# Score parts of 512 keys in four PSUM slots, alternated with the transposed units of a head

## The chip, the cores and the metric

The kernel runs on one core of one Trainium2 chip. The metric is the time of one execution on the device in microseconds (us). TensorE (PE, and PEld for its weight loads), VectorE (DVE), ScalarE (ACT), GpSimd (POOL) and the queue of SyncE (SP) run side by side and meet at semaphores. Each engine takes its own instructions in order.

## The reference, cut to what matters

One decoder block over 2048 tokens: a convolution branch, an attention branch and a SwiGLU feed-forward. The change is in the attention branch. There an indexer picks up to 256 keys for each query; the kernel works on all causal keys and adds a mask instead of gathering:

```
score = where(causal, sum_h w_h * relu(q_idx_h . k_idx), -inf)
idx   = top_k(score, 256)
att   = (q . k[idx]) * 64 ** -0.5 - slopes * distance      # 8 heads, one shared key/value head
p     = softmax(att);  y = p @ v[idx]
```

## The kernel before, in words

The 2048 rows are worked in four groups of 512 rows. A group is `RT` = 4 row tiles of 128 queries. For each group g there are three phases: A (projections, convolution, indexer scores), C (attention and the output projections) and F (feed-forward of the group before). `ORDER` is A0 C0 A1 F0 C1 A2 F1 C2 A3 F2 C3 F3, and PE goes through it in this order. Top-k and the first mask for C run on DVE beside F.

Phase C takes 16 pairs of heads (`PAIRS`): pair i is row tile i // 4 and heads 2(i % 4) and 2(i % 4) + 1; e = 0, 1 is the head in the pair. Row tile t of group g attends to n = 4g + t + 1 key tiles of 128 keys, so 1 to 4 in group 0 and 13 to 16 in group 3. A step (i, e) does this:

- **Scores.** PE multiplies the queries of a head with the keys (L1524 with the high part of the keys, L1525 with the low part, at most 512 keys in one matmul) into one of two score slots of two PSUM banks each (`score_bank`). `parts_of(g)` is 1, 1, 2, 2: a part is up to 1024 keys (`part_span`). PE may write part r when part r - 2 has been read (L1517).
- **Mask and minimum.** DVE reads a part, adds the mask, writes `probs` and keeps the running minimum (L1221). It is a custom instruction followed by a READ_ACCUMULATOR that writes the minimum to `first_top`, or to `mx` for the last part. A later part starts from the earlier minimum, so it waits for it.
- **Exponential.** ACT takes the whole row of keys at once, up to 2048 elements (L796), after the last part of the head.
- **Units.** The probabilities of a pair are transposed on PE in units of two key tiles for both heads (L1480, helper `transposes`), into two banks used by turns. ACT copies the unit (L783: high part), DVE subtracts (L1230: low part), and PE multiplies it with the values (L1499, L1500, helper `values`, two units behind). Transposing unit k waits until DVE is done with unit k - 2, and the first unit of a pair waits for the exponentials of both its heads (`exp_done`, L1475).
- **weigh** (L1187, L1189) is DVE's finish of a pair, three units after its last one. **mark** (L953 to L964) is five DVE steps per pair that prepare the mask of the next row tile. They come behind units, in the pairs with i % 4 <= g of the first three row tiles; such pairs are called marked below.

The units of a pair come `lag` pairs after its scores: 2 in groups 0 and 1, 1 in groups 2 and 3 (`ways`). `slots(g)` lists the units and splits those of a pair over the two steps: in group 3 four units at e = 0 and three or four at e = 1; in group 2 three, and two or three; in group 1 two, and one or two.

All three engines have this order written out. On PE and DVE a step is: all score parts of (i, e), then all units of (i - lag, e). On ACT a step is the other way round: the copies of the units of (i - lag, e) (L773 to L784), and then the exponential of (i, e) (L791 to L797).

Of the kernel before, what the change touches and what calls it, by code (L numbers as in the profile page):

```python
# [23 lines left out]
def build_block(nc, A):  # L24
# [4 lines left out]
    P = 128  # L29
# [8 lines left out]
    RT = ROWS // P  # L38
# [82 lines left out]
    with ctx:  # L121
# [31 lines left out]
        KH = sb("KH", [P, SEQ], f32r)  # L153
        KL = sb("KL", [P, SEQ], f32r)
# [44 lines left out]
        PS = ctx.enter_context(nc.psum_tensor("PS", [P, 8, 512], f32))  # L199
# [22 lines left out]
        mark_step, marked0, marked, m0_ready, m_ready, s_psum, s_masked, exp_done = sem("mark_step"), sem("first_keys_marked"), sem("keys_marked"), sem("first_mask_ready"), sem("mask_ready"), sem("s_psum"), sem("scores_masked"), sem("exp_done")  # L222
# [6 lines left out]
        y_psum, y_copied, y_added, ny_done = sem("y_psum"), sem("y_copied"), sem("y_added"), sem("ny_done")  # L229
# [21 lines left out]
        def slots(g):  # L251

            out, at = [], {}
            for i in range(PAIRS):
                n = RT * g + i // (HEADS // 2) + 1
                mid = min(n, 2 * ((n + 3) // 4))
                for half, (a, z) in enumerate(((0, mid), (mid, n))):
                    at[i, half] = range(len(out), len(out) + (z - a + 1) // 2)
                    out += [(i, k, min(2, z - k)) for k in range(a, z, 2)]
            return out, at  # L260

        PAIRS = RT * HEADS // 2

        PT_BASE = [sum(len(slots(a)[0]) for a in range(g)) for g in range(GROUPS)]

        def parts_of(g):

            return (g + 2) // 2

        PART_BASE = [sum(2 * PAIRS * parts_of(a) for a in range(g)) for g in range(GROUPS)]  # L270

# [3 lines left out]

        def part_span(b, v):

            return 1024 * v, min(1024, (b + 1) * P - 1024 * v)

        def score_bank(r):  # L280

            return PS[:, 2 * (r % 2):2 * (r % 2) + 2, :].rearrange("p a n -> p (a n)")

        def pt_end(g, i):

# [616 lines left out]
        def _(dve):  # L902
# [105 lines left out]
            for ph, g in ORDER:  # L1008
                c0 = BASE[ph, g]
                if ph == "A":  # L1010
# [81 lines left out]
                    for t, b in enumerate(blocks(g)):  # L1092
                        n = (b + 1) * P
# [78 lines left out]
                elif ph == "C":  # L1172
# [4 lines left out]
                    def weigh(k):  # L1177

                        if k < 0 or k != at[table[k][0], 1].stop - 1:
                            return  # L1180
                        i = table[k][0]
                        n = PAIRS * g + i
                        t, j = i // (HEADS // 2), i % (HEADS // 2)
                        o = PS[:, 6 + n % 2, 0:2 * P]
                        dve.wait_ge(bc_done, n + 1)

                        chained(nc.vector.tensor_tensor(out=o[0:DH, :], in0=o[0:DH, :], in1=pvl[:, n % 2, :], op=ALU.add))  # L1187
                        for e in range(2):
                            nc.vector.tensor_tensor(out=att[DH * e:DH * e + DH, j, t * P:(t + 1) * P],  # L1189
                                                    in0=PS[0:DH, 6 + n % 2, e * P:(e + 1) * P], in1=bcs[DH * e:DH * e + DH, n % 2, :],  # L1190
                                                    op=ALU.mult).then_inc(att_done, 1)
# [3 lines left out]
                    for i in range(PAIRS + lag):  # L1195

                        t, u_mark = i // (HEADS // 2) + 1, i % (HEADS // 2)
                        marking = t < RT and u_mark < U
                        step = 0
                        for e in range(2):  # L1200
                            if i < PAIRS:
                                b, h = RT * g + i // (HEADS // 2), 2 * (i % (HEADS // 2)) + e

                                top = mx[:, i % held, e:e + 1]
                                if e == 0 and i >= held:

                                    dve.wait_ge(pt_psum, pt_end(g, i - held))
                                if h == 0 and b % RT == 0:
                                    dve.wait_ge(m0_ready, (g + 1) * (g + 2) // 2)
                                elif h == 0:  # L1210
                                    dve.wait_ge(m_ready, MASK_BASE[g] + b % RT * U)
                                low = 3.0e38
                                for v in range(parts_of(g)):
                                    s, w = part_span(b, v)
                                    r = part(g, i, e, v)
                                    last = v + 1 == parts_of(g)
                                    dve.wait_ge(s_psum, r + 1)
                                    if v:
                                        dve.wait_ge(s_masked, r)
                                    out = top if last else first_top[:, e:e + 1]  # L1220
                                    nc.vector.tensor_tensor_reduce(out=prob(g, i, e)[:, s:s + w], in0=score_bank(r)[:, 0:w],  # L1221
                                                                   in1=M[:, b % RT % 2, s:s + w].bitcast(f32), scale=-2.0 ** -(h + 1),
                                                                   scalar=low, op0=ALU.add, op1=ALU.min, accum_out=out).then_inc(s_masked, 1)
                                    low = out
                            if i >= lag:
                                for k in at[i - lag, e]:

                                    w = table[k][2] * 2 * P
                                    dve.wait_ge(pt_hi, PT_BASE[g] + k + 1)
                                    nc.vector.tensor_tensor(out=pt_hl(g, k, len(table), 1, w), in0=PS[:, 4 + k % 2, 0:w],  # L1230
                                                            in1=pt_hl(g, k, len(table), 0, w).bitcast(f32), op=ALU.subtract).then_inc(pt_ready, 1)
                                    if marking and step < MARKS:
                                        mark(t, RT * g + t, u_mark, step)
                                        step += 1
                                    weigh(k - 3)
                                if e == 0:

                                    n = PAIRS * g + i - lag
                                    dve.wait_ge(exp_done, 2 * n + 2)
                                    if n >= 2:  # L1240

                                        dve.wait_ge(rsb_ready, 2 * n - 2)
                                    nc.vector.reciprocal(rs[:, n % 2, :], den[:, (i - lag) % held, :]).then_inc(recip_done, 1)
                        while marking and step < MARKS:
                            mark(t, RT * g + t, u_mark, step)
                            step += 1
# [61 lines left out]
        def _(pe):  # L1308
# [68 lines left out]
            for ph, g in ORDER:  # L1377
# [83 lines left out]
                elif ph == "C":  # L1461
# [44 lines left out]
                    for i in range(PAIRS + lag):  # L1506
                        for e in range(2):
                            if i < PAIRS:
                                t, h = i // (HEADS // 2), 2 * (i % (HEADS // 2)) + e
                                if g > 0 and t == 0 and e == 0:  # L1510
                                    pe.wait_ge(qs_in[h // 2], 16 * g)
                                lhs = QS[:, h, t * P:(t + 1) * P]
                                for v in range(parts_of(g)):
                                    r = part(g, i, e, v)
                                    s0, w0 = part_span(RT * g + t, v)
                                    if r >= PART_BASE[g] + 2:
                                        pe.wait_ge(s_masked, r - 1)  # L1517
                                    elif g > 0:

                                        pe.wait_ge(ny_done, RT * (g - 1) + r - PART_BASE[g] + 1)  # L1520
                                    for at_s in range(0, w0, 512):
                                        s, w = s0 + at_s, min(512, w0 - at_s)
                                        o = score_bank(r)[:, at_s:at_s + w]
                                        mm(o, lhs, KH[:, s:s + w], start=True, stop=False)  # L1524
                                        ins = mm(o, lhs, KL[:, s:s + w], start=False, stop=True)  # L1525
                                    ins.then_inc(s_psum, 1)
                            if i >= lag:
                                for k in at[i - lag, e]:
                                    transposes(k)
                                    values(k - 2)  # L1530
                    for k in range(len(table) - 2, len(table)):
# [69 lines left out]
```

## Time and profile before

| | |
|---|---|
| median of 3 runs | 3564.96 us (3560.70 to 3566.21) |
| profiled execution, own time | 3566.14 us |
| span in it | 3564.3 us |
| PE busy | 3234.4 us, 91% |
| DVE busy | 2203.8 us, 62% |
| ACT busy | 1188.8 us, 33% |
| attention steps of groups 0, 1, 2, 3 | 345 to 411, 1111 to 1227, 1933 to 2114, 2857 to 3101 us |

Busy times count instructions that work on data. A wait counts for the engine that waits, and "<-" names what ended it. The attention steps of the four groups are 607 us of the span. The rest is mostly PE with matmul after matmul.

### The profile page before, as it was taken

The numbers are of one execution on the slowest core, as the hardware profiler recorded it, in microseconds if no ns is written. First come the engines' busy times: TensorE is split into PE (matmuls) and PEld (weight loads), VectorE is DVE, ScalarE is ACT, GpSimd is POOL, SyncE is SP. The second block draws the span as 40 slices with busy tenths as digits, with TensorE's granted clock in tenths as the row PEclk, the third lists the DMA queues.
The fourth block names the chain that finished last, engine by engine and source line by source line (L and its number), as shares of the span: only waits on it lengthen the run. The fifth ranks groups of instructions, "written<-read, shape, count | busy, mean of one in ns | idle before, by whom it ended". The sixth has DMA issues, their size and how long they took to land.

```text
span 3564.3 us, 41835 instructions
## 1 busy us (share of the span) xinstructions
PE 3234.4 (91%) x15045; PEld 2645.7 (74%) x15045; DVE 2203.8 (62%) x3903; ACT 1188.8 (33%) x2030; POOL 715.3 (20%) x482
## 2 busy tenths in 40 slices
PE   6990799999998899999998789999999867889998
PEld 5860688778886788768887678875888756768886
DVE  1758827588606826699964972759999988720001
ACT  3341641253334641261112653127111056521111
POOL 3420210035766000001212300000221231002212
PEclk9995999999998999999999999999999989999999
DMA  6970465579995265545554035552555410255554
GB/s 216 304 236 0 170 256 201 195 230 291 289 295 181 108 233 197 183 150 193 190 198 160 25 118 224 205 185 98 197 190 196 175 48 1 106 190 195 194 190 170
DMA packets 177567, 640.15 MB, mean 180 GB/s; under 512 B 11294, under 2 KB 95306, under 8 KB 115561
## 3 DMA queue, kind: packets, MB, share of 16 engines
q1 hardware_dynamic: 160512, 574.66, 46.3%
q10 hardware_dynamic: 16872, 63.01, 4.6%
q8 instruction: 121, 1.98, 0.2%
q14 instruction: 62, 0.50, 0.0%
HBM read 476.14 MB, written 161.48 MB: 179 GB/s over the span
## 4 chain that ended last, share of the span: by engine, by line
PE 62%; DVE 17%; issue 12%; ACT 4%; DMA 2%; POOL 2%; DVEq 0%; ACTq 0%; SPq 0%; POOLq 0%
PE PS L1361 14%; PE PS L1332 13%; PE PS L1333 13%; PE PS L1334 13%; DVE probs L1221 3%; DVE flags L1127 2%; DVE W L1112 1%; DVE PT L1230 1%; PE PS L1346 1%; PE PS L1347 1%; PE PS L1348 1%; PE PS L1480 1%; DVE W L1230 1%; DVE ties L955 1%; PE PS L1315 1%
## 5 line engine op out<-in xcount | busy, mean ns | idle before, releaser
L1127 DVE TENSOR_SCALAR_CACHE_REDUCE flags<-W,cand 128x1408 uint8<-128x1408 f32 (+3 forms) x462 | 683.5, 1479 | 53.7 <-DVE cand L1157 39.9
L1361 PE MATMUL PS<-WS,HT 128*128 128x512 f32 x2088 | 483.4, 391 | 5.0 <-POOL WS L442 2.8
L1361 PEld LDWEIGHTS PS<-WS,HT 128*128 128x128 f32 x2088 | 394.0, 189 | 88.4 <-issue 3.6
L1332 PE MATMUL PS<-HF,WS 128*128 128x512 f32 x1072 | 417.4, 389 | 4.1 <-DVE HF L929 2.2
L1334 PE MATMUL PS<-HF,WS 128*128 128x512 f32 x1072 | 417.1, 389 | 0.0
L1333 PE MATMUL PS<-HF,WS 128*128 128x512 f32 x1072 | 417.0, 389 | 0.0
L513 POOL TENSOR_TENSOR TMP<-TMP 128x512 f32<-128x512 f32 x88 | 113.3, 1288 | 1510.8 <-ACT TMP L865 1510.8
L442 POOL TENSOR_TENSOR WS<-RAW,WS 128x1024 fp32r<-128x1024 f32 x116 | 278.2, 2398 | 616.7 <-ACT WS L585 586.9
L1332 PE MATMUL PS<-HT,WS 128*128 128x512 f32 x824 | 325.1, 395 | 1.1 <-POOL WS L442 1.1
L1334 PE MATMUL PS<-HT,WS 128*128 128x512 f32 x824 | 320.8, 389 | 0.0
L1333 PE MATMUL PS<-HT,WS 128*128 128x512 f32 x824 | 320.6, 389 | 0.0
L1480 PE MATMUL PS<-ident,probs 128*128 128x128 f32 x1088 | 182.3, 291 | 107.4 <-DVE PT L1230 62.7
L1524 PE MATMUL PS<-KH,QS 128*128 128x512 f32 (+3 forms) x320 | 133.1, 416 | 122.8 <-DVE mx L1221 83.6
L1297 DVE TENSOR_TENSOR attn<-PS,XR 128x1024 f32<-128x1024 f32 x16 | 18.8, 1219 | 364.2 <-PE PS L1361 364.0
L1332 PEld LDWEIGHTS PS<-HF,WS 128*128 128x128 f32 x1072 | 201.2, 188 | 47.4 <-issue 3.1
L585 ACT ACTIVATE WS<-RAW 128x1024 fp32r<-128x1024 f32 x116 | 122.8, 1059 | 334.8 <-PE PS L1334 163.8
L1334 PEld LDWEIGHTS PS<-HF,WS 128*128 128x128 f32 x1072 | 201.2, 188 | 41.7
L1333 PEld LDWEIGHTS PS<-HF,WS 128*128 128x128 f32 x1072 | 201.2, 188 | 41.7
L1480 PEld LDWEIGHTS PS<-ident,probs 128*128 128x128 f32 x1088 | 130.0, 148 | 136.3 <-issue 112.6
L998 DVE SCALAR_TENSOR_TENSOR PS<-W,cw,PS 128x512 f32<-128x512 f32 x336 | 221.9, 744 | 0.0
L796 ACT ACTIVATE probs<-probs,mx 128x128 f32<-128x128 f32 (+15 forms) x128 | 153.3, 1198 | 100.3 <-DVE mx L1221 100.2
L1361 PE MATMUL PS<-W,HT 128*128 128x512 f32 x792 | 184.9, 389 | 0.0
(220 smaller groups left out, 6106.2 us busy)
## 6 DMA issues: line engine op xcount, KB each, us to landing
WS<-split_weights_scratch SPq DMA_DIRECT2D x234, 1024.0 KB, 4.8
split_weights_scratch<-WS SPq DMA_DIRECT2D x116, 1024.0 KB, 5.0
W<-split_weights_scratch SPq DMA_DIRECT2D x114, 1024.0 KB, 4.8
RAW<-in_w_in SPq DMA_DIRECT2D x34, 512.0 KB, 6.1
RAW<-in_w_ffn_gate SPq DMA_DIRECT2D x22, 512.0 KB, 6.3
RAW<-in_w_ffn_up SPq DMA_DIRECT2D x22, 512.0 KB, 6.3
RAW<-in_w_ffn_down SPq DMA_DIRECT2D x22, 512.0 KB, 5.7
W<-in_x ACTq DMA_DIRECT2D x4, 2048.0 KB, 11.7
```

What stands on the lines that cost most here:

```text
L442: nc.gpsimd.tensor_tensor(out=WS[:, slot, 1, :], in0=RAW[:, slot, :], in1=WS[:, slot, 0, :].bitcast(f32), op=ALU.subtract).then_inc(w_lo, 1)
L513: nc.gpsimd.tensor_tensor(out=TMP[:, s, :], in0=TMP[:, s, :], in1=TMP[:, 2 + s, :], op=ALU.mult).then_inc(h_prod, 1)
L585: nc.scalar.activation(WS[:, slot, 0, :], RAW[:, slot, :], ACT.Copy).then_inc(w_hi, 1)
L796: nc.scalar.activation(row, row, ACT.Exp, bias=mx[:, i % held, e:e + 1], scale=-1.0, accum_out=den[:, i % held, e:e + 1]).then_inc(exp_don ...
L998: nc.vector.scalar_tensor_tensor(out=TAPSUM[:, c, :], in0=GLU[:, c, ds(k0 + i, ROWS)], scalar=cw[:, c, ds(k0 + i, 1)], in1=TAPSUM[:, c, :] ...
L1127: step(nc.vector.tensor_scalar(flags[:, 0:n], SC[:, t, 0:n], cand[:, t:t + 1].bitcast(f32), 0.0, op, ALU.add, accum_out=count[:, t:t + 1]))
L1332: mm(PS[:, bank, :], wh, src[:, 0, k, :], start=k == 0, stop=False)
L1333: mm(PS[:, bank, :], wh, src[:, 1, k, :], start=False, stop=False)
L1334: ins = mm(PS[:, bank, :], wl, src[:, 0, k, :], start=False, stop=k == KD - 1)
L1361: ins = mm(PS[:, 2 * t + half, :], lhs, split(c, w_part)[:, half * 512:(half + 1) * 512], start=first and part == 0 and w_part == 0, stop= ...
L1480: ins = nc.tensor.transpose(PS[:, 4 + k % 2, (2 * a + e) * P:(2 * a + e + 1) * P], prob(g, i, e)[:, (k0 + a) * P:(k0 + a + 1) * P], ident[ ...
L1524: mm(o, lhs, KH[:, s:s + w], start=True, stop=False)
```

## The change

The score area stays PSUM banks 0 to 3, now as four slots of one bank. `parts_of(g)` becomes g + 1 and a part is up to 512 keys. A new helper `woven` cuts the units of a step into as many runs as there are parts, and PE and DVE go through part 0, run 0, part 1, run 1 and so on. PE may write part r when part r - 4 has been read. ACT's order is not touched; its wait for the last part of a head follows `parts_of`.

```diff
+        def woven(g, i, e, lag, at):
+            n = parts_of(g) if i < PAIRS else 0
+            ks = at[i - lag, e] if i >= lag else range(0)
+            if n == 0:
+                return [(None, ks)]
+            cut = [len(ks) * v // n for v in range(n + 1)]
+            return [(v, ks[cut[v]:cut[v + 1]]) for v in range(n)]
...
         def parts_of(g):
-            return (g + 2) // 2
+            return g + 1
...
         def part_span(b, v):
-            return 1024 * v, min(1024, (b + 1) * P - 1024 * v)
+            return 512 * v, min(512, (b + 1) * P - 512 * v)
 
         def score_bank(r):
-            return PS[:, 2 * (r % 2):2 * (r % 2) + 2, :].rearrange("p a n -> p (a n)")
+            return PS[:, r % 4, :]
...
# DVE
-                                for v in range(parts_of(g)):
+                            for v, ks in woven(g, i, e, lag, at):
+                                if v is not None:
...
-                            if i >= lag:
-                                for k in at[i - lag, e]:
+                                for k in ks:
...
                                     weigh(k - 3)
+                            if i >= lag:
                                 if e == 0:
...
# PE
-                                for v in range(parts_of(g)):
+                            for v, ks in woven(g, i, e, lag, at):
+                                if v is not None:
                                     r = part(g, i, e, v)
                                     s0, w0 = part_span(RT * g + t, v)
-                                    if r >= PART_BASE[g] + 2:
-                                        pe.wait_ge(s_masked, r - 1)
+                                    if r >= PART_BASE[g] + 4:
+                                        pe.wait_ge(s_masked, r - 3)
                                     elif g > 0:
-                                        pe.wait_ge(ny_done, RT * (g - 1) + r - PART_BASE[g] + 1)
-                                    for at_s in range(0, w0, 512):
-                                        s, w = s0 + at_s, min(512, w0 - at_s)
-                                        o = score_bank(r)[:, at_s:at_s + w]
-                                        mm(o, lhs, KH[:, s:s + w], start=True, stop=False)
-                                        ins = mm(o, lhs, KL[:, s:s + w], start=False, stop=True)
-                                    ins.then_inc(s_psum, 1)
-                            if i >= lag:
-                                for k in at[i - lag, e]:
+                                        pe.wait_ge(ny_done, RT * (g - 1) + (r - PART_BASE[g]) // 2 + 1)
+                                    o = score_bank(r)[:, 0:w0]
+                                    mm(o, lhs, KH[:, s0:s0 + w0], start=True, stop=False)
+                                    mm(o, lhs, KL[:, s0:s0 + w0], start=False, stop=True).then_inc(s_psum, 1)
+                                for k in ks:
                                     transposes(k)
                                     values(k - 2)
```

## Rows read from the trace of the kernel before

**Rows 1.** Windows of groups 2 and 3: busy of each engine, granted clock, DMA.
```profile
1933.00:2114.00 181.00, 137.57 (x890) 120.99 (x890) 156.66 (x330) 115.33 (x221) 39.45 (x33) 0.94 0.12 45
2857.00:3101.00 244.00, 190.20 (x1208) 167.82 (x1209) 205.29 (x378) 144.89 (x248) 46.96 (x39) 0.92 0.08 31
```
**Rows 2.** Waits in 2857 to 3101 us: total, times, longest.
```profile
DVE probs L1221 <- PE PS L1525: 16.7, 14, 4.7
...
DVE W L1230 <- ACT W L783: 11.0, 20, 1.4
...
DVE PT L1230 <- ACT PT L783: 5.8, 6, 2.6
```
**Rows 3.** Waits in 1933 to 2114 us.
```profile
DVE W L1230 <- ACT W L783: 7.7, 10, 2.7
...
DVE PT L1230 <- ACT PT L783: 6.6, 10, 0.8
...
DVE probs L1221 <- PE PS L1525: 3.3, 7, 0.8
```
**Rows 4.** Waits in 1111 to 1227 us.
```profile
DVE PT L1230 <- ACT PT L783: 3.3, 6, 0.9
...
DVE W L1230 <- ACT W L783: 1.4, 4, 0.7
```
**Rows 5.** Timeline of a pair of group 3, n = 16: start, length, engine, operation.
```profile
3060.36 2.00 ACT L796 ACTIVATE probs<-probs,mx 128x2048 f32<-128x2048 f32 x1
3061.38 1.23 DVE L1221 CUSTOM_DVE_ANT_0 probs<-PS,QI 128x1024 f32<-128x1024 f32 x1 [0.18 <-PE PS L1525]
...
3062.50 0.66 PE L1480 MATMUL PS<-ident,probs 128*128 128x128 f32 x4 [0.37 <-ACT probs L796]
...
3063.20 0.60 ACT L783 ACTIVATE PT<-PS 128x512 fp32r<-128x512 f32 x1 [0.75 <-PE PS L1480]
...
3065.47 0.60 ACT L783 ACTIVATE W<-PS 128x512 fp32r<-128x512 f32 x1 [0.76 <-PE PS L1480]
...
3066.10 0.69 DVE L1230 TENSOR_TENSOR W<-PS,W 128x512 fp32r<-128x512 f32 x1 [0.66 <-ACT W L783]
...
3067.14 2.01 ACT L796 ACTIVATE probs<-probs,mx 128x2048 f32<-128x2048 f32 x1
...
3067.88 0.69 DVE L1230 TENSOR_TENSOR W<-PS,W 128x512 fp32r<-128x512 f32 x1
...
3069.15 0.60 ACT L783 ACTIVATE PT<-PS 128x512 fp32r<-128x512 f32 x1
...
3075.05 1.23 DVE L1221 CUSTOM_DVE_ANT_0 probs<-PS,QI 128x1024 f32<-128x1024 f32 x1 [0.19 <-PE PS L1525]
```
**Rows 6.** Groups by shape: the exponentials, longest and shortest of groups 1 to 3.
```profile
L796 ACT ACTIVATE probs<-probs,mx 128x2048 f32<-128x2048 f32 x8 | 16.0, 2003 | 0.0
...
L796 ACT ACTIVATE probs<-probs,mx 128x640 f32<-128x640 f32 x8 | 6.6, 825 | 3.1 <-DVE mx L1221 3.1
```
**Rows 7.** Timeline of DVE in a step of group 2.
```profile
2089.02 0.08 DVE L1221 DVE_READ_ACCUMULATOR2_ANT first_top<- 128x1 f32 x1
...
2089.25 0.75 DVE L1221 CUSTOM_DVE_ANT_0 probs<-PS,QI,first_top 128x512 f32<-128x512 f32 x1
...
2089.93 0.69 DVE L1230 TENSOR_TENSOR PT<-PS,PT 128x512 fp32r<-128x512 f32 x1
2090.53 0.68 DVE L1230 TENSOR_TENSOR W<-PS,W 128x512 fp32r<-128x512 f32 x1
```
**Rows 8.** Timeline of DVE in group 0: a single part of 512 keys.
```profile
386.73 0.68 DVE L1221 CUSTOM_DVE_ANT_0 probs<-PS,QI 128x512 f32<-128x512 f32 x1
```
**Rows 9.** Timeline of DVE in group 3: one step of mark.
```profile
3013.83 0.74 DVE L964 SCALAR_TENSOR_TENSOR W<-W,cand,ties 128x512 f32<-128x512 f32 x1
```
**Rows 10.** Timeline of PE in group 3: the end of an idle time.
```profile
3014.06 0.63 PE L1480 MATMUL PS<-ident,probs 128*128 128x128 f32 x4 [2.66 <-DVE PT L1230]
```
**Rows 11.** Windows of group 3 just behind it; the granted clock is the third from last.
```profile
3015.70:3019.10 3.40, 3.40 (x12) 2.82 (x11) 1.54 (x3) 2.26 (x3) 0.95 (x1) 0.51 0.02 5
```

## The prediction

> **What bounds the kernel now.** I read the windows over the attention steps first, then the waits inside them, then the timeline of single pairs. The windows show DVE busy for 156.7 of 181.0 us in group 2 and 205.3 of 244.0 in group 3, ahead of PE with 137.6 and 190.2 [rows 1]. So DVE's order sets the pace there and its idle time is what the change could win. The waits say what this idle is: in group 3, 16.7 us behind the scores (4.7 of it once, at the start) and 16.8 behind ACT's copies; in group 2, 14.3 behind copies and 3.3 behind scores; in group 1, 4.7 behind copies [rows 2 to 4]. That is 28.8, 17.6 and 4.7 us, 51 in all, once the start is left out.
>
> The timeline of a pair with n = 16 shows why. From its first score part to that of the next pair it takes 13.67 us (3061.38 to 3075.05). Inside, DVE waits 0.66 us for a copy at 3066.10: the units go round PE, ACT and DVE through two banks, and a round takes longer than two subtractions. The exponential of the head starts at 3067.14, behind the copies, while DVE's score parts of the next step are still to come. At 3062.50 PE waits only 0.37 us for an exponential [rows 5]. So before, ACT's 2 us lie almost whole beside two score parts of DVE.
>
> Attention phases stand in line with the rest on PE, so a microsecond there is one of the total. No DMA, no queue and no instruction of ACT, POOL or SP is moved.
>
> **Part 1: smaller parts.** Parts per head go from 1, 1, 2, 2 to 1, 2, 3, 4, for 32 heads in a group: 32, 32 and 64 more in groups 1, 2 and 3. What one costs DVE comes from issue to issue. A part of 1024 keys takes 1.13 to 1.15 us and one of 512 keys 0.60 (0.68 long, the next starts 0.08 before its end), or 0.68 if it starts from an earlier minimum (2089.25 to 2089.93) [rows 5, 7, 8]. So 1024 keys in two parts cost 0.15 us more. If the later part comes directly behind the earlier, it also pays 0.23 us: the read of the accumulator, 0.08, and 0.15 until the next starts (2089.02 to 2089.25) [rows 7]. A unit in between hides this.
> - Group 1: 32 x 0.15 = 4.8, and 12 heads have no unit between their parts (four before the lag, eight with one unit for two parts): 12 x 0.23 = 2.8. Together +7.6.
> - Group 2: 32 x 0.15 = 4.8; 32 gaps of 0.23 become 12, -4.6. Together +0.2.
> - Group 3: 64 x 0.15 = 9.6; 32 gaps become 14, -4.1. Together +5.5.
>
> All 13.3 us are DVE's, and DVE is the bound. Below, this could be nothing, if it fell into idle time; above, 128 x 0.38 = 49 us, if every part paid its gap. I take 13.3, by the rows nearest to it.
>
> The trace puts the price of a further part of 1024 keys at 0.15 us [rows 5, 7, 8]. The Trainium skill (VectorE: DVE Perf Modes, "The TRN2 errata") has a fixed cost for each instruction that many small tiles pay each time, 120 cycles at 0.96 GHz with a PSUM source. By this the 128 parts would be an estimated 16 us, against 19 by the rows without the saved gaps; rule and rows both speak against the change.
>
> **Part 2: the order, and what it uncovers.** A round of two units on DVE becomes two subtractions and two parts, 2 x 0.60 + 2 x 0.68 = 2.56 us, longer than PE, ACT and back. The first part of a step needs two matmuls and not four, and PE has written it while DVE is at earlier parts. So the 51 us of idle time should go. I let them go whole.
>
> But DVE now reads the last part of a head near the end of its step, with one subtraction behind it and not all. ACT's exponential can start only then, and ACT's next copies queue behind it in order; so do DVE's next subtraction, all of DVE's later parts, and PE's transpose of the next pair, with PE's later parts behind it. DVE has in this time one subtraction, 0.60, and the first part of the next step, 0.60: cover 1.20 us.
> - From e = 1 to e = 0 the chain is: accumulator read 0.08 [rows 7], exponential to transpose 2.14 (3060.36 to 3062.50), transpose to copy 0.70 (to 3063.20), copy to subtraction 0.63 (3065.47 to 3066.10) [rows 5]. That is 3.55 us, so DVE stalls 2.35.
> - From e = 0 to e = 1 no transpose waits, only the copy behind the exponential: 0.08 + 2.01 (3067.14 to 3069.15) + 0.63 = 2.72 us, a stall of 1.52 [rows 5, 7].
>
> Exponentials get shorter by 0.107 us for 128 keys (2.003 at 2048, 0.825 at 640) [rows 6]. The last unit of an odd n is half as wide, some 0.24 us less cover. A step of mark behind the last unit hides 0.66 us of it (0.74 long) [rows 9]; weigh hides 1.08 (3066.10 + 0.69 to 3067.88) [rows 5].
> - Group 3: 15 boundaries e = 1 to 0 at a mean of 2.30: 34.5. The others: 4 x 1.52 for n = 16; n = 15 has a mark behind the last unit: 4 x 0.75; for n = 13, 14 there are three units for four parts, so two parts come first and nothing is left. Sum 43.6.
> - Group 2, e = 1 to 0: n = 12: 3 x 1.92; n = 11: 4 x 2.05; n = 10 and 9 with a mark in three of four pairs: 3 x 1.06 + 1.72 and 3 x 1.19 + 1.85. Sum 24.1. From e = 0 to 1 weigh lies behind the last unit and covers the rest.
> - Group 1: no transpose waits, the lag is two. n = 8: 8 x 0.64; n = 7, the two unmarked pairs: 2 x (0.54 + 0.78). Sum 7.8. n = 5, 6 are covered.
> - Group 0: one part as before. Two more slots let PE run ahead; I count nothing.
>
> The ends: nothing, if ACT were never late; 1.52 + 2.35 for each of 48 pairs = 186 us. I take the sums.
>
> **Sum.** Group 3: 43.6 - 28.8 + 5.5 = 20. Group 2: 24.1 - 17.6 + 0.2 = 7. Group 1: 7.8 - 4.7 + 7.6 = 11. Together +38. A pair of n = 16 checks it: 13.67 before; after, three times 0.60 + 0.68 from first subtraction to last read, twice, is 7.68, with the two chains 6.27 and weigh 1.08: 15.0, so +1.4.
>
> **Part 3: TensorE's clock.** In the trace an idle time of 2.66 us on PE (3014.06) was followed from 3015.70 by 3.40 us at a granted clock of 0.51, the level of 1.2 GHz [rows 10, 11]. In the new order PE has one score part to do before each wait for an exponential and then idles for over 2 us in the pairs of groups 2 and 3. In marked pairs DVE's extra work hides a slower PE. In the 11 unmarked pairs half of 3.4 us is lost on PE and I let 0.7 us of this reach DVE: +8. The ends are 0 and 32 x 1.7 = 54.
>
> So 3566.1 (the profiled execution's own time, 1.8 over its span) + 46 = 3612, and the median of the runs is 1.2 below it: 3611 us.
>
> **The rivals.**
> - *The clock decides.* PE's idle before every pair keeps it at 1.2 GHz for much of groups 2 and 3. If the granted clock falls from 0.93 to 0.80, PE's 328 us [rows 1] become 53 longer; half of this beside DVE leaves +27 on top of the rest: 38 + 8 + 27 = 73, 3638 us. For: the idle time that did it [rows 10, 11]. Against: no score pair shown reaches it for long at 0.92 to 0.94 over a group. The Trainium skill (TensorE: Matmul & The Clock Gate, "A second HAM failure mode: psum-queue depth-cycling") says the same: short idle times between groups of matmuls make the clock swing between its levels; it would give the time of this rival.
> - *Half is covered.* The stall lies where DVE was held anyway, by POOL and by marks that run late, and the parts fall partly into it: +22, 3587 us. For: marked pairs fill most of the time in groups 2 and 3. Against: DVE and ACT are in order, and nothing else is let past.
> - *Faster: the round of units was all.* If ACT's chain stays under DVE's cover, the 51 us of idle are won and 13 paid: -38 at most; with a third of the stalls left (25 us) -13, 3552 us. It decides at a chain of 1.20 us; the shortest exponential alone is 0.83, with copy and start 1.54 [rows 5 to 7]. Only if DVE found other work there would it be so.
> - *No difference.* The loss and gain are equal: needs stalls of 38 us instead of 75.
>
> **How the numbers follow.** Forecast 0.68; clock 0.14; half covered 0.11; faster 0.04; no difference 0.03. The forecast's own range is 3595 to 3630. The range for 8 in 10 takes in most of the second and third case: 3583 to 3645. A run tells a change from none beyond about 0.2%, 7 us. Slower 0.92, same 0.04, faster 0.04.
>
> **What would show it.** After: DVE's largest wait in groups 2 and 3 is L1230 behind ACT's copies L783, about 25 and 45 us in all, with single waits of 1.9 to 2.4 us once a pair, and almost no wait of L1221 behind L1525. ACT's exponentials wait for `mx` where they hardly did. PE's L1480 waits for L796 by 2 us a pair. A pair of n = 16 takes 15.0 us, of n = 12 about the 11 us of before. Group 3 is 20 to 25 us longer, group 1 about 11, group 0 the same. The prediction is wrong if L1230 waits less in group 3 than before, if the stall sits elsewhere (scores late, PE at half clock throughout), or if the groups are longer by less than 19 us together.

## The result and the profile after

The changed kernel takes 3631.42 us (median of 4 runs, 3629.01 to 3636.1) against 3563.03 us before (4 runs): ratio 1.0194, 95% interval 1.0182 to 1.0206, +68 us. The forecast was +46 us and 3611 us. The result lies 1.4 us above the forecast's own range (3595 to 3630) and inside the range for 8 in 10 (3583 to 3645). The span of the profiled execution is 3634.3 us, 70.0 more than before.

All of it lies in the attention steps. The table gives their length, from the first score part on DVE (L1221 before, L1231 after) to the first subtraction of the output (L1254, L1264):

| group | before | after | difference | forecast |
|---|---|---|---|---|
| 0 | 61.9 | 62.7 | +0.7 | 0 |
| 1 | 113.3 | 123.9 | +10.6 | +11 |
| 2 | 179.0 | 206.1 | +27.2 | +7 |
| 3 | 241.5 | 274.3 | +32.8 | +20 |
| clock | | | (in 2 and 3) | +8 |
| sum | 595.6 | 667.0 | +71.4 | +46 |

The windows of the changed kernel over groups 1, 2 and 3 (length, then busy time of PE, weight loads, DVE, ACT and POOL, granted clock, DMA):

```profile
1114.80:1238.70 123.90, 91.76 (x567) 75.41 (x567) 109.17 (x278) 79.71 (x185) 33.16 (x27) 0.90 0.17 67
1946.60:2152.80 206.20, 145.52 (x887) 125.28 (x885) 161.11 (x394) 116.05 (x221) 39.53 (x33) 0.87 0.10 37
2897.10:3171.50 274.40, 201.94 (x1208) 170.99 (x1207) 210.06 (x507) 147.05 (x249) 43.49 (x35) 0.88 0.06 25
```

Against [rows 1], DVE's busy time grew by 4 to 5 us in each of groups 2 and 3, and the windows by 25 and 30: DVE works little more, it waits more. The granted clock fell from 0.94 and 0.92 to 0.87 and 0.88. What DVE and PE wait for, in the same windows of group 2 and then of group 3 (total, times, longest):

```profile
PE PS L1490 <- ACT probs L805: 50.0, 15, 7.5
ACT probs L805 <- DVE mx L1231: 28.1, 20, 4.1
DVE W L1239 <- ACT W L792: 20.8, 19, 2.5
DVE PT L1239 <- ACT PT L792: 17.9, 19, 2.1
...
DVE probs L1231 <- PE PS L1534: 2.5, 6, 0.6
```

```profile
DVE PT L1239 <- ACT PT L792: 45.7, 32, 3.1
ACT probs L805 <- DVE mx L1231: 40.9, 30, 2.8
PE PS L1490 <- ACT probs L805: 37.8, 15, 2.9
...
DVE W L1239 <- ACT W L792: 12.1, 10, 2.7
DVE probs L1231 <- PE PS L1534: 6.0, 6, 3.9
```

DVE's waits behind ACT's copies went from 14.3 to 38.7 us in group 2 and from 16.8 to 57.8 in group 3 [rows 2, 3]; those behind the scores from 16.7 to 6.0 in group 3. PE waits 15 times in each group, once a pair, for exponentials. The timeline of a pair of n = 16 in group 3 (start, length, engine, operation, idle time before and its end) shows the two stalls:

```profile
3116.88 2.01 ACT L805 ACTIVATE probs<-probs,mx 128x2048 f32<-128x2048 f32 x1 [1.24 <-DVE mx L1231]
...
3118.88 0.58 ACT L792 ACTIVATE PT<-PS 128x512 fp32r<-128x512 f32 x1
...
3119.49 0.69 DVE L1239 TENSOR_TENSOR PT<-PS,PT 128x512 fp32r<-128x512 f32 x1 [1.38 <-ACT PT L792]
...
3123.31 0.08 DVE L1231 DVE_READ_ACCUMULATOR2_ANT mx<- 128x1 f32 x1
3123.31 0.69 DVE L1239 TENSOR_TENSOR W<-PS,W 128x512 fp32r<-128x512 f32 x1
3123.42 2.00 ACT L805 ACTIVATE probs<-probs,mx 128x2048 f32<-128x2048 f32 x1 [0.45 <-DVE mx L1231]
3123.91 0.68 DVE L1231 CUSTOM_DVE_ANT_0 probs<-PS,QI 128x512 f32<-128x512 f32 x1
...
3125.57 0.74 PE L1490 MATMUL PS<-ident,probs 128*128 128x128 f32 x4 [2.29 <-ACT probs L805]
...
3126.35 0.60 ACT L792 ACTIVATE PT<-PS 128x512 fp32r<-128x512 f32 x1 [0.83 <-PE PS L1490]
...
3126.98 0.69 DVE L1239 TENSOR_TENSOR PT<-PS,PT 128x512 fp32r<-128x512 f32 x1 [2.38 <-ACT PT L792]
```

Read it downwards from 3123.31. The last part of the second head is done, ACT starts its exponential 0.11 us later, and DVE has one subtraction and one part (3123.31, 3123.91). The transpose follows the exponential at 3125.57, the copy at 3126.35, and DVE goes on at 3126.98 after a stall of 2.38 us. At the other boundary no transpose waits, and the stall is 1.38 (3119.49).

The three pairs of n = 16 took 16.8 to 17.2 us, where 15.0 had been worked out. The long stall before their first subtraction is 2.4 to 2.8 us, and in each two more waits follow it that the working did not have: 0.39 us for a score part and 0.72 for the next copy. With PE kept busy (after_fill below) those two are gone, the stalls are still 2.3 to 2.6 and 1.4, and the pairs take 15.2 to 15.6.

The clock shows in three pairs of n = 12 in group 2. Their windows, one behind the other, each from the first part of a pair to that of the next:

```profile
2094.92:2106.00 11.08, 8.46 (x58) 7.09 (x58) 8.73 (x23) 7.39 (x15) 0.00 (x0) 1.00 0.04 17
2106.00:2119.07 13.07, 10.27 (x60) 8.65 (x60) 9.09 (x24) 7.99 (x15) 0.00 (x0) 0.87 0.00 1
2119.07:2130.50 11.43, 8.92 (x62) 7.55 (x62) 8.99 (x23) 7.71 (x15) 0.00 (x0) 1.00 0.00 1
```

The same work takes 11.08 and 11.43 us at 1.00 and 13.07 at 0.87. Behind PE's idle time in the slow one (first fence, timeline) comes a stretch at the 1.2 GHz level (second, windows):

```profile
2107.51 0.66 PE L1490 MATMUL PS<-ident,probs 128*128 128x128 f32 x4 [2.19 <-ACT probs L805]
```

```profile
2109.00:2112.00 3.00, 3.00 (x13) 2.68 (x12) 2.06 (x5) 0.60 (x1) 0.00 (x0) 0.50 0.00 0
```

### The profile page after: what moved, and what is told of

Same layout as the page of the kernel before. It is cut to its first block, busy times and chain, and to the rows that moved or that the text cites. A ratio compares the mean times of both kernels' runs of the same rounds, so it can differ in the third digit from the quotient of the medians.

```text
span 3634.3 us, 42219 instructions
## 1 busy us (share of the span) xinstructions
PE 3255.5 (90%) x15045; PEld 2650.6 (73%) x15045; DVE 2221.3 (61%) x4159; ACT 1190.0 (33%) x2030; POOL 711.2 (20%) x482
## 3 DMA queue, kind: packets, MB, share of 16 engines
q8 instruction: 121, 1.98, 0.2%
## 4 chain that ended last, share of the span: by engine, by line
PE 61%; DVE 15%; issue 15%; ACT 4%; DMA 2%; POOL 2%; ACTq 0%; DVEq 0%; SPq 0%; POOLq 0%
PE PS L1371 13%; PE PS L1342 13%; PE PS L1344 13%; PE PS L1343 13%; DVE probs L1231 2%; DVE flags L1136 2%; PE PS L1490 2%; DVE W L1121 1%; PE PS L1356 1%; PE PS L1357 1%; PE PS L1358 1%; DVE ties L964 1%; PE PS L1325 1%; DMA RAW<-in_w_in 1%; DVE change L1162 1%
## 5 line engine op out<-in xcount | busy, mean ns | idle before, releaser
L522 POOL TENSOR_TENSOR TMP<-TMP 128x512 f32<-128x512 f32 x88 | 113.3, 1287 | 1538.8 <-ACT TMP L874 1538.8
L1490 PE MATMUL PS<-ident,probs 128*128 128x128 f32 x1088 | 195.3, 306 | 163.3 <-ACT probs L805 88.3
L1490 PEld LDWEIGHTS PS<-ident,probs 128*128 128x128 f32 x1088 | 142.4, 157 | 229.3 <-issue 113.7
```

Of the source, the lines that this page charges most:

```text
L522: nc.gpsimd.tensor_tensor(out=TMP[:, s, :], in0=TMP[:, s, :], in1=TMP[:, 2 + s, :], op=ALU.mult).then_inc(h_prod, 1)
L1490: ins = nc.tensor.transpose(PS[:, 4 + k % 2, (2 * a + e) * P:(2 * a + e + 1) * P], prob(g, i, e)[:, (k0 + a) * P:(k0 + a + 1) * P], ident[ ...
```

## The experiments

Three theories were to be told apart. A: the loss is the exponential that starts late, behind a last part near the end of its step. B: the small parts themselves. C: PE's clock, lowered behind its longer waits. Diffs are against the changed kernel, except that before_fill adds its matmuls to the kernel before. Times are medians, and ratios are to the kernel before as measured beside each. Differences in us below are of medians; by the ratios some come out up to 5 us different. The groups' lengths are read as in the table above, from one profile each.

| kernel | us | ratio (95%) | group 1 | group 2 | group 3 |
|---|---|---|---|---|---|
| parts_only | 3602.54 | 1.0117 (1.0100 to 1.0133) | 117.0 | 192.2 | 260.9 |
| order_only | 3553.12 | 0.9974 (0.9964 to 0.9984) | 113.3 | 179.0 | 228.2 |
| last_early | 3582.91 | 1.0066 (1.0049 to 1.0083) | 116.7 | 185.5 | 247.7 |
| one_between | 3559.41 | 0.9992 (0.9982 to 1.0002) | 112.3 | 183.8 | 234.2 |
| after_fill | 3612.39 | 1.0131 (1.0116 to 1.0147) | 124.1 | 194.0 | 260.9 |
| before_fill | 3579.33 | 1.0046 (1.0031 to 1.0062) | 112.2 | 185.4 | 249.7 |
| order_fill | 3551.46 | 0.9964 (0.9950 to 0.9977) | 111.8 | 182.2 | 231.0 |
| mixed | 3558.80 | 0.9985 (0.9976 to 0.9994) | 110.7 | 180.4 | 237.0 |
| early_e1 | 3610.45 | 1.0135 (1.0118 to 1.0152) | 117.1 | 203.6 | 260.9 |
| early_e0 | 3593.17 | 1.0079 (1.0063 to 1.0096) | 118.8 | 192.9 | 252.5 |

### The parts alone (parts_only)

```diff
-            cut = [len(ks) * v // n for v in range(n + 1)]
+            cut = [0] * n + [len(ks)]
```

> Parts of 512 keys in four slots, but all parts of a step before all of its units, as in the kernel before. Theory A (the loss of the change is the exponential that ACT can start only behind the last part, near the end of the step): here the exponential starts early again, DVE pays 0.15 us for each of 128 further parts and 0.23 for each of 128 gaps, 49 us, of which some 20 fall into its idle time: +30 us against before (+15 to +45), DVE's waits for copies no larger than before. Rival B (the small parts themselves are the loss): as much as the whole change, +68 or more. Rival C (the clock, set off by PE's waits for exponentials): like A, since these waits are gone; granted clock in groups 2 and 3 back at 0.92 to 0.94.

Measured: 3602.54 us, +38 against before and 29 less than the changed kernel. That is inside what A allowed (+15 to +45) and far from B's +68, so the small parts alone are not the loss. They are a part of it: in groups 1 to 3 DVE's busy time is 21 us longer than before and its idle time 14. C was to be like A here, with the clock back, and the clock was not as expected, 0.86 in group 3:

```profile
2876.20:3137.10 260.90, 199.87 (x1208) 177.24 (x1206) 217.69 (x506) 145.19 (x249) 45.14 (x35) 0.86 0.07 27
```

A low clock alone therefore does not need waits for exponentials. In this kernel's window PE waits 40.2 and 16.0 us for DVE's subtractions, and only 2.2 for exponentials. The mean clock does not rank the kernels either: this group is 13 us shorter than that of the changed kernel, at a lower clock.

```profile
PE PS L1490 <- DVE PT L1239: 40.2, 23, 4.5
PE PS L1490 <- DVE W L1239: 16.0, 12, 3.3
...
PE PS L1490 <- ACT probs L805: 2.2, 2, 1.8
```

### The order alone (order_only)

`parts_of`, `part_span`, `score_bank`, the two waits and the matmul loop as before the change; only `woven` stays. Its halves put one or two units between two parts of up to 1024 keys:

```diff
         def parts_of(g):
-            return g + 1
+            return (g + 2) // 2
...
         def score_bank(r):
-            return PS[:, r % 4, :]
+            return PS[:, 2 * (r % 2):2 * (r % 2) + 2, :].rearrange("p a n -> p (a n)")
```

> Parts of 1024 keys in two slots as before, but part 0, half of the units, part 1, the other half, in groups 2 and 3. Theory A: behind the last part of a head lie now two subtractions and then a part of 1024 keys, 2.3 us of cover against a chain of 3.55 (n = 16), so stalls of 1.2 us once a pair, less than the idle time before plus nothing for parts, with the gaps of 0.23 gone: 0 us against before (-12 to +12). Rival B: 0 or faster. If alternation as such is the loss: over +30.

Measured: 3553.12 us, 11 less than before (interval 0.9964 to 0.9984), at the fast end of what A said; B allowed it too (0 or faster), so this run does not tell A from B. Alternation as such costs nothing; with larger parts it gains, all of it in group 3, where the clock is 0.97. DVE's waits for copies and scores in groups 1 to 3 hardly fell, from 59.5 to 58.7 us. What fell is its other idle time, from 16.0 to 7.2, where the gaps between two parts of a head lie, and in group 3 its busy time, by 5:

```profile
1934.10:2113.10 179.00, 136.42 (x885) 117.70 (x884) 155.58 (x328) 115.02 (x221) 39.11 (x33) 0.92 0.11 42
2858.40:3086.60 228.20, 179.80 (x1206) 154.35 (x1204) 200.69 (x379) 146.47 (x249) 44.26 (x32) 0.97 0.07 29
```

### The last part one place earlier (last_early)

```diff
-            cut = [len(ks) * v // n for v in range(n + 1)]
+            cut = [0] + [min(v, len(ks)) for v in range(n - 1)] + [len(ks)]
```

> The changed kernel with the runs of units moved back by one part: part 0, part 1, unit 0, part 2, unit 1, part 3, then the last two units (group 3); group 1 has both parts before its units. Only the places differ from the changed kernel. Theory A: cover behind the last part grows from 1.20 to 2.7 us, stalls in group 3 from 2.35 to 0.85 a pair, in group 2 to between 0.45 and 1.0: +5 us against before (-5 to +20), that is some 60 us faster than the changed kernel, with what is left in group 1 (+12). Rival B: +60 or more, as the parts are the same. Rival C: PE's waits for exponentials shrink, clock back at 0.92 to 0.94 in groups 2 and 3; it can't be told from A by this time alone.

Measured: 3582.91 us, 48.5 less than the changed kernel with the same parts, slots and instructions, only in other places; A had said some 60. PE's wait for exponentials in group 3 fell from 37.8 to 23.8 us, DVE's for copies from 57.8 to 26.1:

```profile
PE PS L1490 <- ACT probs L805: 23.8, 14, 2.4
...
DVE PT L1239 <- ACT PT L792: 18.3, 16, 3.0
...
DVE W L1239 <- ACT W L792: 7.8, 11, 1.3
```

B's +60 or more against before did not come. This shows A, with the clock's part in it, since that came back to 0.91 and 0.93 in groups 2 and 3 with the shorter waits. Against order_only it is 30 us slower, 3.5, 6.5 and 19.5 in groups 1, 2 and 3. That is at most the price of 128 more parts, 0.23 us each: the places of the parts differ too, and in group 3 the clock (0.93 against 0.97). DVE's busy time accounts for 18 of it.

### One unit between large parts (one_between)

```diff
-            cut = [len(ks) * v // n for v in range(n + 1)]
+            cut = [0] + [1] * (n - 1) + [len(ks)]
```

with the parts of order_only.

> Parts of 1024 keys in two slots as before, one unit between part 0 and part 1 and the rest behind part 1, in groups 2 and 3. Theory A: cover behind the last part of three subtractions and a part of 1024, 2.9 us (group 3), two and a part in group 2, 2.3; the gap of 0.23 us between parts is hidden 60 times: -10 us against before (-20 to +3). Rival B gives the same sign. If any alternation on PE costs by itself: slower than before.

Measured: 3559.41 us, 5 less than before and not told from no change by its interval. In group 2 its order of work is the very one of order_only, since a half of two or three units is one; but its window took 183.8 us at 0.88, against 179.0 at 0.92:

```profile
1933.90:2117.70 183.80, 142.96 (x885) 124.76 (x884) 154.82 (x329) 114.77 (x221) 40.08 (x33) 0.88 0.10 40
```

So 5 us in one group of one profile come about without any change of the order; the clock is what differs with it. Group 1 is the same program in order_only and mixed, and took 113.3 and 110.7 us. For group 3 (234.2 against 228.2) this leaves open whether one unit is worse than two.

### PE kept busy (after_fill, before_fill, order_fill)

```diff
+                        if g >= 2 and k0 == 0 and 0 < i < PAIRS - 1:
+                            pe.wait_ge(pt_ready, PT_BASE[g] + k - 1)
+                            for _ in range(6):
+                                mm(PS[:, 4 + k % 2, :], QS[:, 0, 0:P], KH[:, 0:512], start=True, stop=True)
                         pe.wait_ge(exp_done, 2 * (PAIRS * g + i + 1))
```

> The changed kernel, with six matmuls of 512 columns (1.4 us at 2.4 GHz), whose result nothing uses, on PE before each wait of a pair's first transpose for its exponentials, in groups 2 and 3. They fill the idle time. Theory C (half clock behind these waits makes up what the sum of stalls leaves open, some 25 to 30 us): granted clock in groups 2 and 3 from 0.87 back to 0.93 or more, -15 to -30 us against the changed kernel, so 3601 to 3616. Theory A alone (the stalls, whatever the clock): the matmuls end inside the waits or a little late, 0 to +10 us against the changed kernel.

Measured: 3612.39 us. Work was added to PE, and the kernel is 19 us faster than the changed one. Group 2 took 12.1 and group 3 13.4 us less, at 0.96 and 0.95:

```profile
1949.41:2143.42 194.01, 154.64 (x971) 127.84 (x969) 159.42 (x393) 116.68 (x221) 39.62 (x33) 0.96 0.10 39
2886.80:3147.72 260.92, 206.50 (x1292) 170.41 (x1290) 208.85 (x506) 147.17 (x249) 44.82 (x37) 0.95 0.07 29
```

A alone said 0 to +10; so C holds beside A: 25 us in the two groups, 21 in the whole profiled execution and 19 in the medians. It is not the exact price of the lower clock, since what the matmuls delay is in it, and the clock came above the 0.94 and 0.92 of before.

> The same six matmuls in the kernel before, as a control. Its PE waits little at this place (0.4 us in an unmarked pair), so they delay the transpose by about 1 us in those pairs and fill idle time in marked ones. Theory C: the clock in groups 2 and 3 rises from 0.93, gain and delay about cancel: -8 to +12 us. Theory A alone: +10 to +25.

Measured: 3579.33 us, +14 against before, the clock in groups 2 and 3 at 0.94 and 0.93. The control goes the other way, just outside what C allowed (-8 to +12) and inside what A alone said (+10 to +25): where PE hardly waits for exponentials (11 us in groups 2 and 3 before, 88 in the changed kernel), the same matmuls are a delay. Their gain above is tied to the waits that the change made.

> Parts of 1024 keys, half of the units between them (as in order_only), with the six matmuls. Theory C: group 2, at 0.92, gains up to 5 us, group 3 is at 0.97 already and may lose a little: -6 to +6 us against order_only (3553). Theory A alone: +5 to +15.

Measured: 3551.46 us, 1.7 less than order_only; the intervals (0.9950 to 0.9977 and 0.9964 to 0.9984) overlap, so no difference is shown. C had said -6 to +6, A alone +5 to +15.

### One unit or two, by head (mixed)

```diff
-            cut = [len(ks) * v // n for v in range(n + 1)]
+            cut = [0] + [min(2 - e, len(ks))] * (n - 1) + [len(ks)]
```

with the parts of order_only.

> As order_only, but two units between the parts at e = 0, where the chain to the next subtraction is 2.72 us, and one at e = 1, where it is 3.55. Theory A: at e = 1 of n = 15, 16 one subtraction more behind the last part, -0.6 us in 8 pairs if nothing else is late; group 2 at e = 0 has one less behind the last part, with weigh there as cover. -8 to +3 us against order_only (3553).

Measured: 3558.80 us, 5.7 slower than order_only where -8 to +3 was expected: a miss. Group 3 took 237.0 us at a clock of 0.94. Whether the clock came first or the order did is not settled.

### The move in one kind of step only (early_e1, early_e0)

```diff
             cut = [len(ks) * v // n for v in range(n + 1)]
+            if e == 1:
+                cut = [0] + [min(v, len(ks)) for v in range(n - 1)] + [len(ks)]
```

and the same with `e == 0`.

> The changed kernel, with the runs of units moved back by one part only in the steps e = 1, so that two units and not one lie behind the last part of the second head of a pair. Theory A with the chain of 3.55 us: the stall before a pair's first subtraction falls from 2.3 to 0.85 us in 15 pairs of group 3 (-22), from 1.6 to about 0.7 in group 2 (-14), by some 0.7 us in 8 pairs of group 1 (-5); some 28 gaps of 0.23 us come back (+6), and half of what the clock costs goes (-12): -47 us against the changed kernel, 3584 (3575 to 3600). If both boundaries counted alike: about -27, 3604.

> The same only in the steps e = 0, so behind the last part of the first head of a pair. Theory A with the chain of 2.72 us, with marks and weigh as further cover: -9 us in group 3, nothing in group 2, -5 in group 1, some 40 gaps of 0.23 us back (+9), the clock not better, since PE's wait for the exponentials of a pair stays: -5 us against the changed kernel, 3626 (3615 to 3636). If both boundaries counted alike: about -27, 3604.

Measured: 3610.45 us for e = 1 and 3593.17 us for e = 0, so -21 and -38 against the changed kernel where -47 and -5 had been expected. The miss was mine in both, for two reasons. The first is how many steps each edit changes. A step whose units are one fewer than its parts is cut the same way with and without the shift. So of the steps e = 0 the edit changes 14, 15 and 15 in groups 1, 2 and 3, and of the steps e = 1 only 6, 7 and 7; the expectation of -22 us in group 3 had counted 15 of these. The pairs of group 3 show it (sums of their lengths, from first part to first part; pair i carries the units of pair i - 1):

| pairs of group 3 | changed kernel | early_e1 | early_e0 |
|---|---|---|---|
| 1 to 8 (units of n = 13, 14) | 128.5 | 128.1 | 121.8 |
| 9 to 14 (units of n = 15, 16) | 105.6 | 96.5 | 91.3 |

Where early_e1 changes nothing it gained nothing, and where it acts it gained 9.1 us in 6 pairs, 1.5 each, the size that had been expected for one boundary. That early_e0 is the faster kernel comes first from this: 44 changed steps against 20. The second reason is the count of cover. These are the two stalls of a pair of n = 16 in group 3, in early_e1 and then in early_e0:

```profile
3107.85 0.69 DVE L1241 TENSOR_TENSOR PT<-PS,PT 128x512 fp32r<-128x512 f32 x1 [2.03 <-ACT PT L794]
...
3116.01 0.69 DVE L1241 TENSOR_TENSOR PT<-PS,PT 128x512 fp32r<-128x512 f32 x1 [0.47 <-ACT PT L794]
```

```profile
3091.79 0.69 DVE L1241 TENSOR_TENSOR PT<-PS,PT 128x512 fp32r<-128x512 f32 x1 [1.40 <-ACT PT L794]
...
3098.42 0.69 DVE L1241 TENSOR_TENSOR PT<-PS,PT 128x512 fp32r<-128x512 f32 x1 [0.51 <-ACT PT L794]
```

A step that is shifted has two parts in front of its first unit and, with four units for four parts, one more unit behind its last part. The first covers the stall at its own beginning by 0.23 + 0.68 = 0.91 us, the second the stall at its end by 0.60. I had put both at its end. Put right, the long stall of 2.38 becomes 2.38 - 0.60 = 1.78 for e = 1 and 2.38 - 0.91 = 1.47 for e = 0 (measured 2.03 and 1.40), the short one of 1.38 becomes 0.47 and 0.78 (measured 0.47 and 0.51). So the chain and its cover hold, and the count of cover must take both sides of the boundary. By this the stalls of such a pair fall by 1.9 us for e = 0 and by 1.3 for e = 1. In group 2, early_e1 changed little (203.6 against 206.1): half of its steps e = 1 have two units for three parts and stay as they were.

## Why the prediction was right or wrong

**The bound: right.** DVE's waits tell the result. Over groups 1 to 3 the changed kernel has 118 us of waits of DVE behind ACT's copies and PE's scores (13.0, 41.2 and 63.8), and the kernel before 59.5 (8.4, 17.6 and 33.5), all counted with their first waits: +58. Busy time grew by 14 us (3.6, 6.3, 4.5, in windows cut at the first score part and the first output subtraction). DVE's other idle time, where the gaps lie, fell by 4. The sum is 69 against 71 measured.

**Part 1, the price of parts: right within 3 us.** 13.3 us were forecast, 19 for the parts less 6 for gaps. Measured are 14 us more of busy time, in which the steps of mark are 4 shorter, and 4 less of other idle time: 10 in all. Against order_only with the last part early, and against before with no unit between the parts, the kernels with these parts are 30 and 38 us slower, other effects included; the bounds that were given were 0 and 49.

**Part 2, the uncovered exponential: right in place and size.** The stalls were put at 2.35 and 1.52 us and measured 2.38 and 1.38 in the pair shown, 2.4 to 2.8 and 1.38 in the pairs of n = 16. last_early shows that the place of the last part is the cause: -48.5 us with nothing but places changed. Group 1 came out at +10.6 against +11, in part by luck: its waits for copies and scores grew by 4.6 us where +3.1 was the balance of the terms, and the parts cost less than their 7.6. At the higher clock of after_fill groups 2 and 3 are 15.0 and 19.4 us above before, against 7 and 20 forecast: the idle time of before was credited in full, and in group 2 the filled kernel still has 30 us of waits behind copies against 24 forecast. No run shows the 51 us gone whole: after_fill has 94 us of waits for copies and scores in groups 1 to 3, against 80 for the forecast stalls and the start, and order_only has 58.7 against 59.5 before. (The terms of group 2 add up to 24.3 and not 24.1, which changes nothing.)

**Part 3, the clock: the mis-sized term.** +8 was forecast; after_fill puts it at 25 us in the two groups. The step that failed is that "in marked pairs DVE's extra work hides a slower PE". It does not: pairs 5 to 7 of group 2 (counted from 0) took 13.80, 12.26 and 11.96 us in the changed kernel and 12.45, 11.36 and 9.55 with PE kept busy, and the first two of them are marked. Pairs 5 and 6, in the changed kernel and then in after_fill:

```profile
2001.92:2015.72 13.80, 8.92 (x52) 7.95 (x52) 11.08 (x29) 7.17 (x14) 1.90 (x2) 0.84 0.02 7
2015.72:2027.98 12.26, 8.91 (x54) 7.96 (x54) 10.30 (x28) 6.57 (x14) 1.90 (x2) 0.82 0.01 1
```

```profile
2003.41:2015.86 12.45, 8.94 (x58) 7.36 (x58) 10.91 (x29) 7.18 (x14) 1.91 (x2) 1.00 0.03 9
2015.86:2027.22 11.36, 9.00 (x60) 7.59 (x60) 10.12 (x28) 6.79 (x14) 1.90 (x2) 1.00 0.00 0
```

Over groups 2 and 3, 14.0 of the 25.5 us came back in marked pairs, where the forecast had nothing, and 11.6 in the 11 unmarked ones, 1.05 each where it had 0.7. In the marked pairs PE waits for the exponentials of a pair for up to 7.5 us and then starts at the lower level, and transpose, copy and subtraction of the first units are on the chain that DVE waits for. The rival on the clock is nearer to the result than the forecast, +73 against a measured +68, and its mechanism is the one that was under-priced; but the clock of 0.80 by which it came to this was not reached, and a part of what it made up for is idle time of before that was credited in full. That 3631 lies in the range for 8 in 10 is owed to the room that this rival was given; the forecast's own sum was 20 us short.

**The other rivals.** That the round of units was all is refuted for this order and yet has its truth: with large parts (order_only) the alternation gains 11 us. It won them from the gaps between parts and from busy time, not from the waits for copies and scores that it was meant for; the small parts and the late last part cost more than this. "Half is covered" fell with the stalls at their full size.

## What to carry to other kernels

Before two streams of an engine are interleaved, ask what a third engine starts only behind the last piece of one of them. Its length must fit under what the first engine has left on both sides of the boundary, here 1.2 us under a chain of 3.55. Interleave so that the last piece comes early, and keep the pieces as large as the buffers allow: the same alternation was 11 us faster than before with two parts of 1024 keys and 68 us slower with four of 512 and the last one late. Then look at what the new waits do to PE's clock, pair by pair.

## What the runs showed of the hardware that was not expected

- Adding 84 matmuls, whose result nothing uses, to each of two groups made the changed kernel 19 us faster and the kernel before 14 us slower. The granted clock rose from 0.87 and 0.88 to 0.96 and 0.95 in the first.
- An idle time of PE of 2.19 us was followed by 3 us at 0.50, and a pair of the same kernel with the same work passed at 1.00: 13.07 and 11.08 us. Of two idle times of 1.98 us of PE in pairs of n = 12, one (its end at 2120.3) had 5 us at 1.00 behind it, the other (2131.7) 3.4 us at 0.54 from 2133.0.
- The same instructions of group 2 took 179.0 us at 0.92 in one kernel and 183.8 at 0.88 in another.
- Four slots of one bank in place of two of two banks, with everything else the same, made group 0 slower by 0.7 us (61.9 to 62.7) in each of the profiles with them. One profile without them (order_fill) had 63.3, at a clock of 0.79 in this group, so whether the slots did it is open.
